# The gate projections in seven products of half size, two of the four sums of weights on GpSimd

## The reference, cut to what matters

```
h = rmsnorm(x, norm_pre) * (1 + scale) + shift
u = h @ w_in          # q_a k_a v_a z_a q_m k_m v_m o_m z_m i_m f_m g_a g_m, side by side
y_a = (rmsnorm(att) * (1 - lam_init) * silu(z_a)) @ w_br_a
y_m = (sigmoid(o_m) * hm * silu(z_m)) @ w_br_m
y = (sigmoid(g_a) * y_a + sigmoid(g_m) * y_m) @ w_out
out = x + gate * rmsnorm(y, norm_post)
```

## Time and profile before

| | |
|---|---|
| median of the runs | 1974.29 us |
| profiled execution: span from first to last instruction | 1972.5 us |
| PE busy | 1936.3 us, 98% |
| weight loads of PE busy | 1661.0 us, 84% |
| DVE busy | 785.2 us, 40% |
| ACT busy | 641.6 us, 33% |
| POOL busy | 178.6 us, 9% |
| chain of waits that ended last | PE 93%, SP's queue 2%, DVE 2% |
| mean granted TensorE clock | 0.998 of full speed |
| mean DMA rate | 122 GB/s |

### The profile page before, as it was taken

How to read it: one execution, slowest core, us unless ns; L and a number is a source line. 1 busy time by engine, 2 the same in 40 slices (tenths; PEclk the granted TensorE clock), 3 DMA queues, 4 the chain that set the end, 5 groups by cost and what they waited for, 6 DMA issues and landing times.

```text
span 1972.5 us, 31158 instructions
## 1 busy us (share of the span) xinstructions
PE 1936.3 (98%) x12229; PEld 1661.0 (84%) x12229; DVE 785.2 (40%) x1679; ACT 641.6 (33%) x1144; POOL 178.6 (9%) x308
## 2 busy tenths in 40 slices
PE   6999999999999999999999999999999999999997
PEld 4789899988899998889899988878878878878885
DVE  4665324256653345454444322322232232352224
ACT  4222212235545554343343322212222212333332
POOL 2120012000020101132330000000000000010001
PEclk9999999999999999999999999999999999999999
DMA  9995662331234542333343222232232233353223
GB/s 310 325 297 175 205 225 80 80 102 54 54 124 145 180 128 71 78 84 110 99 128 84 80 81 83 83 104 81 80 104 82 84 101 84 122 191 96 80 82 122
DMA packets 166595, 240.52 MB, mean 122 GB/s; under 512 B 15145, under 2 KB 113577, under 8 KB 165305
## 3 DMA queue, kind: packets, MB, share of 16 engines
q1 hardware_dynamic: 150960, 194.03, 32.6%
q0 software_dynamic: 13264, 44.50, 6.8%
q10 hardware_dynamic: 2242, 0.19, 0.1%
HBM read 220.93 MB, written 17.73 MB: 121 GB/s over the span
## 4 chain that ended last, share of the span: by engine, by line
PE 93%; SPq 2%; DVE 2%; DMA 1%; issue 1%; POOL 1%; ACT 1%; DVEq 0%; ACTq 0%
PE gemm L546 75%; PE bank_s L546 9%; PE bank_a L546 3%; PE bank_o L546 2%; SPq L438 2%; DMA ada_in<-in_w_ada 1%; PE bank_s L799 1%; DVE g_m L2052 1%; DVE y_tok L2133 1%; PE bank_s L575 0%; PE bank_a L743 0%; DMA w_raw<-in_w_in 0%; PE bank_s L964 0%; POOL hm_sq L2350 0%; PE bank_s L1076 0%
## 5 line engine op out<-in xcount | busy, mean ns | idle before, releaser
L1518 DVE TENSOR_TENSOR w_lo<-w_raw,w_hi 128x512 fp32r<-128x512 f32 x512 | 358.5, 701 | 777.0 <-ACT w_hi L1153 776.5
L546 PE MATMUL gemm<-h_hi,w_hi 128*128 128x288 f32 (+1 forms) x2560 | 661.6, 324 | 2.9 <-DVE g_m L2052 1.7
L1153 ACT ACTIVATE w_hi<-w_raw 128x512 fp32r<-128x512 f32 x512 | 322.3, 630 | 1021.2 <-PE bank_s L546 568.8
L546 PE MATMUL gemm<-h_hi,w_lo 128*128 128x288 f32 (+1 forms) x2560 | 638.4, 315 | 0.0
L546 PE MATMUL gemm<-h_lo,w_hi 128*128 128x288 f32 (+1 forms) x2560 | 637.5, 314 | 0.0
L546 PEld LDWEIGHTS gemm<-h_hi,w_hi 128*128 128x128 f32 x2560 | 424.4, 189 | 80.7 <-issue 43.1
L546 PEld LDWEIGHTS gemm<-h_lo,w_hi 128*128 128x128 f32 x2560 | 424.9, 188 | 21.1
L546 PEld LDWEIGHTS gemm<-h_hi,w_lo 128*128 128x128 f32 x2560 | 425.3, 188 | 20.3
L546 PE MATMUL gemm<-w_hi,y_all 128*128 128x512 f32 x512 | 158.8, 391 | 0.6 <-DVE g_m L2052 0.6
L546 PEld LDWEIGHTS gemm<-w_hi,y_all 128*128 128x128 f32 x512 | 95.6, 188 | 24.9 <-DVE g_m L2052 1.4
L546 PE MATMUL gemm<-w_lo,y_all 128*128 128x512 f32 x256 | 99.9, 390 | 0.0
(11 more groups left out here) (464 smaller groups left out, 1750.7 us busy)
## 6 DMA issues: line engine op xcount, KB each, us to landing
w_raw<-in_w_in SPq DMA_DIRECT2D x384, 256.0 KB, 2.8
ada_in<-in_w_ada SPq DMA_DIRECT2D x72, 512.0 KB, 7.7
w_raw<-in_w_out SPq DMA_DIRECT2D x64, 256.0 KB, 2.4
ada_gate<-in_w_ada SPq DMA_DIRECT2D x16, 512.0 KB, 5.1
k_page<-in_cache_k POOLq DMA_DIRECT2D x16, 512.0 KB, 5.6
v_page<-in_cache_v POOLq DMA_DIRECT2D x16, 512.0 KB, 4.5
w_raw<-in_w_br_a SPq DMA_DIRECT2D x32, 256.0 KB, 2.4
w_raw<-in_w_br_m SPq DMA_DIRECT2D x32, 256.0 KB, 2.4
```

The source lines that it names most:

```text
L546: return nc.tensor.matmul(out, lhsT, rhs, start=start, stop=stop, skip_group_check=True)
L1153: return nc.scalar.activation(out, in_, func, **kw)
L1518: V.tensor_tensor(w_lo[:, slot], w_raw[:, slot], w_hi[:, slot], ALU.subtract).then_inc(lo_ready, 1)
```

## The change

The 4096 gate columns leave the quads and get a stage of their own between stage 1 and the quads: 16 blocks (i) of 256 columns, 8 granules (j) each, 128 in all. A granule is again 2 kt by 256 columns, seen as a 2 by 2 matrix of 128 by 128 tiles; the tokens are cut into two halves of 288, which with the two kt gives a 2 by 2 matrix too. The scheme of seven products (Strassen's, in Winograd's order) makes the 2 by 2 product with seven products instead of eight, so PE has 7 x 3 = 21 matmuls of 288 columns, each product in a bank of its own (`p_banks`), summed over the eight granules of a block.

- Sums of weights: the four are made for every pair of granules (b): two on DVE in one instruction (`forms_a`), two on POOL, one after the other (`forms_b`). ACT then rounds the seven tiles in one instruction of 896 columns (`form_hi`), DVE takes the rest (`form_lo`). `w_all` (loaded weights and sums) and `f_hi`, `f_lo` have three slots each.
- Sums of `h`: made once, in groups 28 to 31, by DVE and ACT (`sums`, 8 times three steps) in place of the splits of `att` and `z_act`.
- At a block's end ACT copies the first product and DVE joins the seven by seven instructions of 288 columns (`products_a`, `products_b`); the last two banks are not free until the sixth and seventh. A tanh follows, and POOL stores the gates in DRAM (`gate_store`).
- `att` and the `z_m` products are kept in DRAM and read back when `bra` and `brm` are made, at the end of the new stage and in quad 0. The quads have 16 granules each, and the gates are loaded for each quad by two DMAs (`ga_load`, `gm_load`) of 1.18 MB.

The diff, cut to its core:

```diff
...
+WRING = 3
+FORMS = 7
+S_AT = 28 * NG + 6
...
+            def form_load(b):
+                i, k = b // 4, b % 4
+                if b >= WRING:
+                    sp.wait_ge(lo_ready, S_W + 2 * (b - WRING) + 2)
+                elif b == 0:
+                    sp.wait_ge(prod_ready, 4)
+                elif b == 1:
+                    sp.wait_ge(lo_ready, S_W)
+                else:
+                    sp.wait_ge(prod_ready, 8)
+                col = COL_GA + i * CW
...
+            for b in range(GG // 2):
+                form_load(b)
...
+            def form_granule(g):
+                i, j = g // NG, g % NG
+                pe.wait_ge(lo_ready, S_W + g + 1)
+                if not i:
+                    pe.wait_ge(s_lo_made, S_LO + j + 1)
+                wh, wl = f_hi[wslot_of(g)], f_lo[wslot_of(g)]
...
+                order = ((0, h_hi[:, 2 * j, half_a], h_lo[:, 2 * j, half_a]), (5, s_hi[j][:, 1, :], s_lo[j][:, 1, :]),
+                         (2, h_hi[:, 2 * j + 1, half_a], h_lo[:, 2 * j + 1, half_a]), (4, s_hi[j][:, 2, :], s_lo[j][:, 2, :]),
+                         (6, h_hi[:, 2 * j + 1, half_b], h_lo[:, 2 * j + 1, half_b]), (3, s_hi[j][:, 0, :], s_lo[j][:, 0, :]),
+                         (1, s_hi[j][:, 3, :], s4_lo))
+                for k, (of, hi, lo) in enumerate(order):
+                    if j == 0:
+                        if i and not k:
+                            pe.wait_ge(p1_kept, P1_KEPT + i)
+                        elif i:
+                            pe.wait_ge(p_free, 7 * (i - 1) + p_waits[k])
+                        elif k >= 4:
+                            pe.wait_ge(bank_free[k // 6], V0 + 32)
+                    cols = slice(of * P, (of + 1) * P)
+                    for n, (w, h) in enumerate(((wh, hi), (wh, lo), (wl, hi))):
+                        done = mm(p_banks[k], w[:, cols], h, start=j == 0 and n == 0, stop=j == NG - 1 and n == 2)
+                    if j == NG - 1 and k < 6:
+                        done.then_inc(p_done, 1)
+                done.then_inc(gemm_used, 1)
...
-                        pe.wait_ge(bank_free[b // 2], V0 + 32 + (2 * m - 1 + b % 2 if m else 0))
+                        if m:
+                            pe.wait_ge(bank_free[b // 2], V0 + 32 + 2 * m - 1 + b % 2)
+                        else:
+                            pe.wait_ge(p_free, 7 * GP)
...
-                    if j == 2 * KT and not i:
-                        pe.wait_ge(br_lo, 16)
-                    of = h_parts(kt) if kind in ("ga", "gm") else parts(bra if kind == "ya" else brm, kt)
-                    wide_granule(m, j % RING, of, kt == 0, kt == n - 1)
+                    if not i:
+                        pe.wait_ge(br_lo, j + 1)
...
+            def form_hi(g):
+                act.wait_ge(t_made, T_MADE + g // 2 + 1)
+                if g >= WRING:
+                    act.wait_ge(gemm_used, S_W + g - WRING + 1)
+                elif g:
+                    act.wait_ge(gemm_used, S_W - 4 + 2 * g)
+                go(f_hi[wslot_of(g)][:], w_all[g // 2 % WRING][:, g % 2, P:8 * P]).then_inc(hi_ready, 1)
+            for x in range(28 * NG, 32 * NG):
+                p, g = x // NG, x % NG
+                j, r = divmod(x - S_AT, 3)
+                if 0 <= j < NG and r == 2:
+                    act.wait_ge(sums_made, S_MADE + j + 1)
+                    go(s_hi[j][:], s_new[:]).then_inc(s_hi_made, 1)
...
+            for g in range(GG):
+                i, j = g // NG, g % NG
+                if j == NG - 1:
+                    act.wait_ge(p_done, 6 * i + 1)
+                    if i:
+                        act.wait_ge(p_free, 7 * (i - 1) + 2)
+                    go(h_free[:, 14, HALF:T], bank_s[:, 0, 0:HALF]).then_inc(p1_kept, 1)
+                if g + 2 < GG:
+                    form_hi(g + 2)
+                if j == 1 and i:
+                    act.wait_ge(p_free, 7 * i)
+                    c4 = h_free[:].rearrange("p (k e) t -> p k e t", e=2)[:, 0:4, 0, HALF:T]
+                    go(c4, c4, ACT.Tanh, scale=0.5).then_inc(g_tanh, 1)
+                if g >= GG - 6:
+                    br_hi_of(g - GG + 6)
+                if g >= GG - 2:
+                    split_first(S_F + g - GG + 2)
...
+            def sums(j, r):
+                if r == 0:
+                    if j == 0:
                         dve.wait_ge(n_outs, 16 * HM)
                         dve.wait_ge(mst_out, 32 * HM)
...
+                        dve.wait_ge(c_outs[1], 64 * HM)
+                    V.tensor_tensor(s_t_even[:], h_hi[:, 2 * j, :], h_lo[:, 2 * j, :], ALU.add)
+                    link(V.tensor_tensor(s_t_odd[:], h_hi[:, 2 * j + 1, :], h_lo[:, 2 * j + 1, :], ALU.add))
+                if r == 1:
+                    V.tensor_tensor(s_new[:, 0, :], s_t_even[:, HALF:T], s_t_odd[:, HALF:T], ALU.add)
+                    link(V.tensor_tensor(s_new[:, 2, :], s_t_even[:, 0:HALF], s_t_even[:, HALF:T], ALU.subtract))
+                    link(V.tensor_tensor(s_new[:, 1, :], s_new[:, 0, :], s_t_even[:, 0:HALF], ALU.subtract))
+                    V.tensor_tensor(s_new[:, 3, :], s_t_odd[:, 0:HALF], s_new[:, 1, :], ALU.subtract).then_inc(sums_made, 1)
+                if r == 2:
+                    dve.wait_ge(s_hi_made, S_HI + j + 1)
...
+            def forms_a(b):
+                dve.wait_ge(w_ready[b % WRING], W_READY + 32 * (b // WRING + 1))
+                w = w_all[b % WRING][:].rearrange("p s (f c) -> p s f c", c=P)
+                V.tensor_tensor(w[:, :, 4:6, :], w[:, :, 1:3, :], w[:, :, 0:1, :].to_broadcast([P, 2, 2, P]), ALU.subtract).then_inc(t_first, 1)
+            def form_lo(g):
+                dve.wait_ge(hi_ready, S_W + g + 1)
+                V.tensor_tensor(f_lo[wslot_of(g)][:], w_all[g // 2 % WRING][:, g % 2, P:8 * P], f_hi[wslot_of(g)][:], ALU.subtract).then_inc(lo_ready, 1)
...
+            def products_a(i):
+                dve.wait_ge(p1_kept, P1_KEPT + i + 1)
+                dve.wait_ge(p_done, 6 * i + 2)
+                V.tensor_tensor(u2, p1, p6, ALU.add).then_inc(p_free, 1)
+                if i:
+                    dve.wait_ge(g_out, G_OUT + 32 * i)
+                dve.wait_ge(p_done, 6 * i + 3)
+                V.tensor_tensor(c_part(1, 0), p1, p2, ALU.add).then_inc(p_free, 1)
+                dve.wait_ge(p_done, 6 * i + 4)
+                dve.wait_ge(p_free, 7 * i + 1)
+                V.tensor_tensor(u3, u2, p7, ALU.add).then_inc(p_free, 1)
+            def products_b(i):
+                dve.wait_ge(p_done, 6 * i + 5)
+                dve.wait_ge(p_free, 7 * i + 3)
+                V.tensor_tensor(c_part(1, 1), u3, p4, ALU.add).then_inc(p_free, 1)
+                dve.wait_ge(p_done, 6 * i + 6)
+                V.tensor_tensor(c_part(0, 1), u3, p5, ALU.subtract).then_inc(p_free, 1)
+                V.tensor_tensor(u4, u2, p5, ALU.subtract).then_inc(p_free, 1)
+                dve.wait_ge(gemm_used, S_W + NG * (i + 1))
+                dve.wait_ge(p_free, 7 * i + 6)
+                V.tensor_tensor(c_part(0, 0), u4, p3, ALU.add).then_inc(p_free, 1)
...
+                p, g = x // NG, x % NG
+                j, r = divmod(x - S_AT, 3)
+                if x + LOOKAHEAD < S_W:
+                    ahead(p, g)
+                if x == S_W - 3:
+                    forms_a(0)
+                if x == S_W - 2:
+                    dve.wait_ge(s_lo_made, S_LO + NG)
+                    form_lo(0)
+                if x == S_W - 1:
+                    form_lo(1)
+                if 0 <= j < NG:
+                    sums(j, r)
...
+            forms_a(1)
+            for g in range(GG):
+                i, j = g // NG, g % NG
+                b = (g + 3) // 2
+                if g % 2 and b < GG // 2:
+                    forms_a(b)
+                if j == NG - 1:
+                    products_a(i)
+                if g + 2 < GG:
+                    form_lo(g + 2)
+                if j == NG - 1:
+                    products_b(i)
+                if g >= GG - 6:
+                    br_lo_of(g - GG + 6)
+                if g >= GG - 2:
+                    split_lo(slot_of(S_F + g - GG + 2), S_F + g - GG + 2)
+            split_lo(slot_of(S_F + 2), S_F + 2)
...
+            pool.dma_start(att_scratch.rearrange("b p t -> p b t"), att[:]).then_inc(att_out, 16)
...
+            def forms_b(b):
+                pool.wait_ge(t_first, T_FIRST + b + 1)
+                w = w_all[b % WRING][:].rearrange("p s (f c) -> p s f c", c=P)
+                link(G.tensor_tensor(w[:, :, 6, :], w[:, :, 2, :], w[:, :, 4, :], ALU.add))
+                G.tensor_tensor(w[:, :, 7, :], w[:, :, 3, :], w[:, :, 6, :], ALU.subtract).then_inc(t_made, 1)
+            forms_b(0)
+            pool.wait_ge(prod_ready, 8)
+            for blk in range(6, 8):
+                pool.dma_start(prod_scratch[blk], z_act[:, blk % 2, :]).then_inc(p_out, 16)
+            forms_b(1)
+            pool.wait_ge(att_out, AT_OUT + 16)
+            pool.wait_ge(p_out, P_OUT + 128)
```

(23 more changed lines are left out.)

292 lines of the change are left out of this document (183 added, 109 removed).

## The result

| | runs | median | lowest to highest |
|---|---|---|---|
| before | 4 | 1974.51 us | 1973.72 to 1976.00 |
| changed | 4 | 1951.62 us | 1950.38 to 1953.25 |

The ratio of the two is 0.9884, with a 95% interval from 0.9870 to 0.9898: 22.9 us or 1.2% faster. A gain of 46 us was forecast; the time lies in the range of the prediction, at its upper end. The profiled execution has a span of 1948.9 us, against a forecast of 1926.5.

A forecast was written before the change was run, and what follows sets the result against it. PE, busy 98% of the span, was taken as the bound. -54.0 + 2.9 + 1.5 + 1.5 + 2.1 = -46.0 us took the span from 1972.5 to 1926.5, so a median of 1928, range 1917 to 1952.

The forecast's parts named there:

- What goes from PE, -54.0: Gate granules of 2.80 us against 3.192, times 128: -50.2; eight gate matrices lose their fold: -3.5; first bank wait: -0.3.
- The engines beside it, cost 0: Gate stage: ACT, DVE and POOL work per pair of granules hides behind 5.60 us of PE; cost 0.
- 5.17 of 5.60 us: DVE and POOL work per pair, added up as if port-sharing operations go one after the other, against PE's 5.60 us.
- The two rivals on the port: Gate stage: shared port costs more (1973, halfway 1942; chance 0.12); DVE and POOL in turn set the pace (2039; 0.08).
- Item 1: Groups 28 to 30: sums of `h` on DVE stand before its `z_act` work and free banks late, +2.9 us.
- Item 2: Start of the gate stage: PE waits for the first forms, behind two POOL DMA issues, +1.5 us.
- Item 3: 15 block ends: DVE's seventh join frees a bank just in time, 0.1 us each, +1.5 us.
- Item 4: End of the gate stage: first quad granule waits for block 15's joins, behind `bra` blocks, +2.1 us, between 1.4 and 5.
- Item 5: Quads: gates stored and reloaded from DRAM arrive in time; cost 0, margin a few us, three times.
- the gates return late: Rival: gm and ga load in sequence, ga some 7 us late in three quads; +22, 1950 us; chance 0.10.
- an idle PE behind `mix`: Sign, in quads 1 to 3, that would show the forecast wrong through the gates' return.
- 212.6 + 2.1: Quads: 64 granules of 3.192 us plus 11.8 - 3.5 us of matrix ends, 212.6; the 2.1 is item 4.

The follow-up runs named there:

- Experiment 6: Changed kernel plus an eighth product per granule (three more matmuls into the unused bank, result unread): span 1996.5 us.
- experiment 13: Experiment 8, POOL's share kept, `forms_a` half a pair earlier except `forms_a(2)`, `forms_a(1)` before last `z_act` work, POOL's pair-2 forms before attention loads: median 1920.30 us.
- Experiments 4: Changed kernel with each of POOL's two sums of weights made twice: span 2025.6 us.
- experiment 9: Experiment 4's kernel (POOL's sums made twice) with `forms_a` issued half a pair earlier: span 1963.5 us.
- 10: Experiment 9's kernel with each of POOL's sums made three times, six POOL operations per pair: span 2045.9 us.
- experiment 8: Experiment 7 plus quad 0 starting in the free bank, POOL's pair-2 forms before its last product stores, `h` sums off group ends: median 1926.60 us.
- experiment 5: Changed kernel with all four sums of weights on VectorE, none on POOL: median 1945.47 us.
- experiment 3: Changed kernel with eight buffers instead of two for returning products, loaded ahead of quad 0's gates: median 1949.90 us.
- Experiments 2: Changed kernel with y split straight from the gate buffer, never leaving SBUF, and a second pair of gate buffers: median 1939.44 us.
- 7: Changed kernel with the edits of experiments 2 and 3 together (y kept in SBUF, eight product buffers): median 1931.69 us.
- experiments 11: Experiment 8 with all four sums of weights on VectorE and `forms_a(1)` ahead of the last group's `z_act` work: median 1920.34 us.
- 11 to 13: Experiments 11, 13 and 12, which is experiment 13 with `forms_a(2)` ahead of pair 1's low parts: median 1924.28 us for 12.

## Why the prediction was wrong

- **What goes from PE, -54.0: right.** Experiment 6 shows the price of a product. From the first gate matmul to the first out granule experiment 13 takes 570.2 us, where the kernel before has 625.0 from the end of stage 1: 54.8 less, with 1.1 us of waits at the stage's start still in it and granules 0.015 us shorter than forecast.
- **The engines beside it, cost 0: right in size, partly for another reason.** `form_lo` took 1.09 us where it met nothing, `form_hi` 0.95, a POOL sum 0.74 (1.12, 0.93 and 0.72 forecast); blocks kept PE's pace. But the sum 5.17 of 5.60 us was not the right test of the margin. Experiments 4 and 9 show that the chain through the engines decides first, and the collision alone (10) is a little milder than strict turns. The two rivals on the port did not come.
- **Item 1, groups 28 to 30, +2.9: right** (+2.6; gone in experiment 8 when the steps left the group ends).
- **Item 2, start, +1.5: too small.** The wait was 2.9 us, and about 1.4 us of half clock followed it (granule at 1139.46 to the next at 1143.63 are 4.17 us). POOL's two issues were not back to back, as the step had them: 1.07 us of idle time lie between them (1134.12 to 1135.19). The code has one wait, ahead of both, and the profile names nothing that ended this idle time, so its cause stays open.
- **Item 3, block ends, +1.5: nothing came**, and granules took 2.785 instead of 2.80: together 3.4 us better than forecast.
- **Item 4, "the joins end 2.1 us behind PE": mis-sized, and half of it missing.** PE waited 3.96 us, within the 1.4 to 5 given; some 2.5 us of it come with POOL's share of the sums (1.5 us in experiment 5). But quad 0 was 7 us too long: the product blocks, whose return stands in no item, came back in two buffers behind 2.4 MB of gates (2.6 us in experiment 3; 6.5 from 2 to 7), and the wait was followed by half clock (4.3 us for wait and clock, from 7 to 8).
- **Item 5 is the step that failed.** It reads "Gates back from DRAM. ... 0, but the margin is a few us, three times." In quads 1 and 3 the gates did come in time, in quad 2 only nearly: in DVE's timeline `mix` starts at 1632.25 behind 1.15 us of idle time that the load of `g_a` ended, and the matrix took 26.5 us instead of 26.0. The rival "the gates return late" gave a time of 1950, near the measured one, for a reason that cost 0.5 us: its nearness is luck. Its sign, an idle PE behind `mix`, did show in quad 3 (5.2 us), but `mix` stood there behind `y` blocks. What failed is that the step followed the gates alone through the queue they stand in. Before, two gate matrices of 51 us each lay between the last `y_store` and the first `y_hi`. The change removes those matrices, and `y_load(0)` keeps its place behind `y_store(2)`, `gm_load(3)`, a wait and `ga_load(3)`, and is issued at 1677.6 when ACT is there at 1671.2. ACT waits in order, and so a wait of 14.2 us became 13.6 us of quad 3 (66.8 against 53.2). Experiments 2 and 7 show it: without the trip quad 3 takes 53.1 to 53.2 us.

In sum, of the 22.4 us between the forecast and the measured span the quads hold 19.9 (234.6 against 212.6 + 2.1). The gate stage itself took 361.7 us where its terms say 361.4. The rest, 2.2 us, is that it began later, and this is no more than the late start of group 28 (1023.4 against 1021.1), whose variation is as large. That these sums come out so near has luck in it: quad 0 varies by 4 us between executions.

## What to carry to other kernels

When a change removes work from the engine that bounds, list every transfer that the removed work used to cover, not only those that the change touches, and walk each one through its issuing queue up to the engine that waits for it in order. One late block in the queue of an otherwise idle engine stops the bounding engine once the lead of its ring is used up, and the lower clock behind the wait adds to it. When work is given to a second engine only to relieve a first that has time to spare, it may gain nothing, as here, and its queue becomes one more place to be late; a sum of busy times does not see that, a chain through all engines for one step of the loop does.

## What was not expected of the hardware

- Half clock behind short waits: after idle times of 3.8 to 5.2 us PE ran for some 3 to 5 us at the lower level (427 ns per 512 columns); windows of 4 us that it fills in part show 0.56 to 0.68. After waits of 1.1 and 0.7 us the clock stayed at 1.00. In between both occur: it fell behind 2.9 us at the stage's start, behind 2.6 us there in experiment 8 and behind 2.5 us in quad 0 of experiment 6, and it stayed at 1.00 behind 2.3 us in quad 0 of the changed kernel and behind 3.0 us in that of experiment 9.
- A GpSimd sum of 2 x 128 columns takes 0.74 us against 0.425 on VectorE. When they meet, a sum goes from 0.73 to between 1.06 and 1.58 and `form_lo` from 1.09 to between 1.29 and 1.62 (experiments 9 and 10); in 10, six sums per pair and 2.6 us of VectorE's work took 7.03 us.
- The Trainium skill (Perfetto Trace Analysis, "Optimizing Scalar/DVE Operations") says that moving work between GpSimd and VectorE might not help because they share a port. Here the medians of experiments 11 and 13 are 1920.34 and 1920.30 us, with neither engine near its limit.
- Code that depends on returns from DRAM varied by 4.2 us in quad 0 (56.6 to 60.8) between the profiles of seven kernels with the same code there; in experiments 8 and 11 to 13, where the two chains of returns are gone, the sum of the quads is 209.9 to 210.0 us.
- A load of 288 KB on POOL's queue behind two of 1.18 MB took 7.8 us from its issue at 1677.62 until ACT could go on at 1685.43; by itself such a load takes 3.1 us in the kernel before.
